# A two-block transformer on one core: in its mixers, a half chunk between the up projections, one gate product ahead of a weight's low part, and the first merged turns ahead of the last branch half

## Chip, cores, metric

One core of a Trainium2 chip runs the whole program. The metric is the device time of one execution in microseconds (us), lower is better.

## What is computed

The input is one sequence of 256 tokens of width 1024 in float32. A first block of two layers is followed by a second block of two layers. The change lies in the token mixer, which each layer of the first block has once:

```
def token_mixer(hn, ...):
    proj = hn @ w_in
    moba_qkv, sb_qkv, c_q, c_kv, k_rope, gates = split(proj)
    y_a = moba_attention(rope(qa), rope(ka), va)
    y_b = stick_breaking_attention(qb, kb, vb)
    qc = rms_norm(c_q, q_norm) @ w_uq
    kv = rms_norm(c_kv, kv_norm) @ w_ukv
    y_c = causal_softmax_attention(qc, [k_nope, rope(k_rope)], vc)
    g = sigmoid(gates + b_gate)
    merged = sum over the 3 branches of (ys @ w_branch) * g
    return merged @ w_out
```

Around it stand, in each layer, two dense feed-forward parts, norms, modulation by a conditioning vector, and gated residuals. The second block has attention and a mixture of 16 experts, and is not touched.

## The kernel before, in words

Every engine has its own instruction stream, written out by hand; semaphores tie them together. The plan is a list of steps (norm, ffn, mixer, backT, out, resid and so on) that each engine walks through in the same order. `b` holds the counts of each semaphore at the start of a step.

Weights arrive as chunks of 128 x 2048 floats (1 MB), by SP's DMA queue, in a ring of six staging buffers. A matmul in full precision is made of three in a reduced one, so each chunk is taken apart first: ACT rounds it to `w_hi` (`hi(n)`, line 699), DVE subtracts that and rounds the rest to `w_lo` (`lo(n)`, line 1363), each for three chunks at a time (PARTS = 3). `chunk_ready` counts the chunks whose low part is done, `pe_used` the chunks PE is through with. Activations are split in the same way (`hT_hi`, `hT_lo`, `yT_hi`, `yT_lo`). `mm3` (lines 2314, 2317, 2318) issues the three matmuls: high by high, high by low weight, low by high weight.

In the mixer chunks 0 to 33 are counted from `b["n"]`. Three places matter here.

**The up projections.** PE multiplies chunks 0 to 3 (latents and the first 512 columns), then `up_q` (chunk 4) for both token tiles, one into two banks of `acc`, one into `gu`, then `up_kv` (chunk 5) into the same banks. Each has to wait until ACT has copied out what `up_q` left there (`pre_out`). Then come chunks 6 and 7, each in two halves, one for each token tile (`half(c, t, ...)`, 12 matmuls into bank `acc[:, 2 + t]`), with turns (transposes) of q and k among them (`m_turns`). ACT's stream has `hi` of chunks 5 and 6, the copies of `up_q` and `up_kv` in PE's order, and behind them `hi` of chunks 7 and 8. DVE's has `lo` of 5 and 6, the rotary products, `lo` of 7, then copies of turned pieces with `lo` of 8 among them. `half_used` counts first halves done, and ACT waits on it before it copies.

**The slots.** 24 slots of attention heads follow. In slot `s_` PE does a head's scores, weights and outputs, and fills in chunk 8 + `s_` by halves (`fill(s_, 0)`, `fill(s_, 1)`). `MIX_FILL` says what a chunk is: "J" a projection, "G" half of a gate's chunk pair, "B" a branch's output. DVE takes each finished sum out of its bank: `take_block(s_, t)` adds the bias for a gate, or, for a branch, multiplies by the gate (line 2063) and adds to the sum over branches (line 2066). PE may write a bank again when `fill_out[t]` has counted that. In slot 19 the block is ("B", 0, 1). There, as in every slot, DVE's `lo(n0 + 8 + s_ + 2)`, here of chunk 29, stands ahead of `take_block(s_, 0)`, and `take_block` is what frees the bank for `fill(20, 0)`. ACT, ahead of chunk 29's high part, does a sigmoid with two loads of its table.

**The end.** After the slots come chunks 32 and 33 (branch 1, two column halves; `MIX_FILL` 24 and 25). `take_block` of them completes `tok`, the merged sum, and counts `mg_ready`, four in all. Step `backT` turns the first half of the columns (rounds 0 and 1, line 2454), which ACT copies out as `hT_hi` (line 777) and DVE as `hT_lo` (line 1396). Step `out` multiplies by w_out: `high_rows` (16 matmuls, line 2431, two banks for each token tile), `low_rows` (8, line 2441), turn rounds 2 and 3, then `rows` of the next chunk. DVE's stream there: `take_block(24, 0)`, `take_block(24, 1)`, `lo` of chunk 34, `take_block(25, 0)`, `take_block(25, 1)`, `lo` of chunk 35, then the low parts of the turns.

Of the kernel before, what the change touches and what calls it, by code (L numbers as in the profile page):

```python
# [16 lines left out]
NT = S // P  # L17
# [279 lines left out]
def build(nc, wstream, ada_stream, c_in, xin, const_in, vec_in, bgate_in, lam_in, rbias_in, t5_in, rel_in, rw_in, out):  # L297
# [14 lines left out]
    with ExitStack() as ctx:  # L312
# [1036 lines left out]
        def _(dve):  # L1349
# [586 lines left out]
            def mixer(b, l):  # L1936
# [144 lines left out]
                for s_ in range(SLOT_HEADS):  # L2081
# [3 lines left out]
                    if s_ == 0:  # L2085
                        divide(0)
                    if s_ < SLOT_HEADS - 1:
                        lo(n0 + MIX_PRE + s_ + 2)
# [4 lines left out]
                    if s_ == SLOT_HEADS - 1:  # L2093
                        argument(s_)
                    if mine:
                        take_block(s_, 0)
# [214 lines left out]
        def _(pe):  # L2311
# [8 lines left out]
            def chunk_wait(n, i=0, rounds=1):  # L2320
                pe.wait_ge(chunk_ready, n + 1 + STAGES * rounds * i)
# [95 lines left out]
            def merged(r):  # L2417

                return [tok[:, t, (2 * r + k) * P:(2 * r + k + 1) * P] for k in range(2) for t in range(NT)]

            def high_rows(n, lhs, turned):

                pe.wait_ge(th_ready, turned)
                chunk_wait(n)
                s = n % PARTS
                for t in range(NT):
                    for k in range(2):
                        for h in range(2):
                            c = slice(k * D + h * 512, k * D + (h + 1) * 512)
                            for w in (w_hi, w_lo):  # L2430
                                pe.matmul(acc[:, 2 * t + h, :], lhs(k, t)[0], w[:, s, c], start=k == 0 and w is w_hi, stop=False,
                                          skip_group_check=True)
# [548 lines left out]
            def mixer(b, l):  # L2981
# [9 lines left out]

                def half(c, t, dst, k0, first, last, src=(hT_hi, hT_lo)):

                    n = n0 + c
                    if t == 0:
                        chunk_wait(n)
                    for k in range(4):
                        cols = slice(k * 512, (k + 1) * 512)
                        ins = mm3(dst, *(v[:, k0 + k, t * P:(t + 1) * P] for v in src), w_hi[:, n % PARTS, cols],
                                  w_lo[:, n % PARTS, cols], first and k == 0, last and k == 3)  # L3000
                    ins.then_inc(pe_used if t else half_used, 1)

# [31 lines left out]
                up_q(1, gu)  # L3034
                chunk_wait(n0 + 5)
                pe.wait_ge(pre_out, b["po"] + 3)
                up_kv(0, acc[:, 0:2, :])
                pe.wait_ge(pre_out, b["po"] + 4)
                up_kv(1, gu)
                half(6, 0, acc[:, 2, :], 0, True, False)  # L3040
                half(6, 1, acc[:, 3, :], 0, True, False)
                pe.wait_ge(rope_ready, 3 * l + 1)
                m_turns(0)
                half(7, 0, acc[:, 2, :], 4, False, True)
                m_turns(2)
# [118 lines left out]
                for s_ in range(SLOT_HEADS, len(MIX_FILL)):  # L3164
                    for t in range(NT):
                        fill(s_, t)

            pe.nop().then_inc(pe_used, PARTS)
            pe.wait_ge(ld, 16 * N_LD)
            for step, b in plan:  # L3170
# [18 lines left out]
                elif kind == "mixer":  # L3189
                    mixer(b, step[1])  # L3190
                elif kind == "backT":
                    pe.wait_ge(mg_ready, b["mg"])
                    for r in range(2):
                        turn(b["u"] + r, merged(r))
                elif kind == "out":
                    def of(c):
                        return lambda k, t: tuple(v[:, 2 * c + k, t * P:(t + 1) * P] for v in (hT_hi, hT_lo))

                    high_rows(b["n"], of(0), b["th"] - 3)
                    pe.wait_ge(tr_free, b["u"] - 1)  # L3200
                    low_rows(b["n"], of(0))
                    for r in range(2, 4):
                        turn(b["u"] - 4 + r, merged(r))
# [222 lines left out]
```

## Time and profile before

| | |
|---|---|
| median of 3 runs | 2117.34 us (2117.26 to 2125.36) |
| the profiled execution | 2117.01 us |
| its span | 2115.2 us |
| mean granted TensorE clock | 0.979 of full speed |
| PE busy (matmuls) | 1975.3 us, 93% |
| DVE busy | 1381.0 us, 65% |
| ACT busy | 848.7 us, 40% |
| chain that ended last | PE 79%, DVE 9%, ACT 5%, DMA 3%, issue 3% |

The span runs from the first to the last instruction; the execution's time has 1.8 us more around it. The share of an engine is its busy time over the span. The first mixer lies between about 240 and 500 us of the span, the second between about 895 and 1160 us.

### The profile page before, as it was taken

To read this page: it belongs to the slowest core of one execution; us is meant where nothing else is said; L and a number is where in the kernel's file an instruction comes from. 1 tells how busy PE (TensorE), PEld (TensorE's weight loads), DVE (VectorE), ACT (ScalarE), POOL (GpSimd) and SP (SyncE) were. 2 spreads that over 40 slices of the span, in tenths; PEclk is the share of its full clock that TensorE was granted. 3 is DMA by queue.
4 is the path that set the end of the run, shared out by engine and by line. 5 is a ranking of instruction groups with operands and counts; after the bars stand their busy time and mean duration, and the time that the engine had idled before them with its cause. 6 is when DMAs were issued, how large, how long until landed. Compare 5 with 4: busy or idle time off the path is not lost.

```text
span 2115.2 us, 25821 instructions
## 1 busy us (share of the span) xinstructions
PE 1975.3 (93%) x9588; PEld 1443.4 (68%) x9588; DVE 1381.0 (65%) x2202; ACT 848.7 (40%) x1127; POOL 63.7 (3%) x95
## 2 busy tenths in 40 slices
PE   3999999998999999999999999998799989889998
PEld 2788777776888788778777788776544447764443
DVE  6899776767888798876776888776511146642112
ACT  3343555655433543464654444564200035421000
POOL 0000000000000000000000000020000001000000
PEclk9999999999999999999999999999899999989999
DMA  9999444435897799754444799762999996359997
GB/s 396 377 372 376 185 174 156 158 125 228 334 372 301 286 365 368 269 189 160 155 145 149 300 368 382 209 225 97 311 422 421 421 350 242 120 217 422 421 421 318
DMA packets 98176, 597.88 MB, mean 283 GB/s; under 512 B 20240, under 2 KB 23696, under 8 KB 27408
## 3 DMA queue, kind: packets, MB, share of 16 engines
q1 hardware_dynamic: 91600, 585.18, 71.2%
q10 hardware_dynamic: 6464, 11.15, 1.6%
q8 instruction: 76, 1.25, 0.2%
q14 instruction: 36, 0.29, 0.0%
HBM read 595.21 MB, written 1.09 MB: 282 GB/s over the span
## 4 chain that ended last, share of the span: by engine, by line
PE 79%; DVE 9%; ACT 5%; DMA 3%; issue 3%; POOL 1%; ACTq 0%; DVEq 0%; POOLq 0%; SPq 0%
PE gu L2704 11%; PE acc L2314 10%; PE acc L2318 10%; PE acc L2317 10%; PE gu L2314 7%; PE tr L2704 7%; PE gu L2318 7%; PE gu L2317 7%; PE tr L2454 3%; PE acc L2704 3%; ACT w_hi L699 2%; DVE w_lo L1363 2%; DMA more_proj<-wstream 1%; DVE tf L2168 1%; DMA lam<-lam_in 1%
## 5 line engine op out<-in xcount | busy, mean ns | idle before, releaser
L1363 DVE TENSOR_TENSOR w_lo<-stage,w_hi 128x2048 fp32r<-128x2048 f32 x232 | 530.4, 2290 | 90.3 <-ACT w_hi L699 89.9
L699 ACT ACTIVATE w_hi<-stage 128x2048 fp32r<-128x2048 f32 x232 | 442.7, 1913 | 210.2 <-PE acc L2318 204.0
L1428 DVE SCALAR_TENSOR_TENSOR proj<-proj,c_row 128x1024 f32<-128x1024 f32 x240 | 292.1, 1221 | 37.3 <-DMA proj<-ada_stream 26.5
L2314 PE MATMUL acc<-w_hi,hT_hi 128*128 128x512 f32 x656 | 270.6, 412 | 5.9 <-DVE z_mix L2063 2.8
L2314 PE MATMUL gu<-w_hi,hT_hi 128*128 128x512 f32 x656 | 261.4, 399 | 13.1 <-DVE pair L1498 10.7
L2318 PE MATMUL acc<-w_hi,hT_lo 128*128 128x512 f32 x656 | 258.1, 393 | 0.0
L2317 PE MATMUL acc<-w_lo,hT_hi 128*128 128x512 f32 x656 | 257.7, 393 | 0.0
L2318 PE MATMUL gu<-w_hi,hT_lo 128*128 128x512 f32 x656 | 257.1, 392 | 0.0
L2317 PE MATMUL gu<-w_lo,hT_hi 128*128 128x512 f32 x656 | 257.0, 392 | 0.0
L2314 PE MATMUL acc<-w_hi,yT_hi 128*128 128x512 f32 (+1 forms) x460 | 180.8, 393 | 2.8 <-ACT proj L1143 2.7
L2318 PE MATMUL acc<-w_hi,yT_lo 128*128 128x512 f32 (+1 forms) x460 | 178.8, 389 | 0.0
L2317 PE MATMUL acc<-w_lo,yT_hi 128*128 128x512 f32 (+1 forms) x460 | 178.6, 388 | 0.0
L2314 PEld LDWEIGHTS gu<-w_hi,hT_hi 128*128 128x128 f32 x656 | 124.0, 189 | 40.5 <-DVE pair L1498 13.2
L2314 PEld LDWEIGHTS acc<-w_hi,hT_hi 128*128 128x128 f32 x656 | 124.4, 190 | 38.9 <-issue 6.6
L2318 PEld LDWEIGHTS acc<-w_hi,hT_lo 128*128 128x128 f32 x656 | 124.3, 189 | 27.7
L2318 PEld LDWEIGHTS gu<-w_hi,hT_lo 128*128 128x128 f32 x656 | 124.0, 189 | 26.7
L2317 PEld LDWEIGHTS gu<-w_lo,hT_hi 128*128 128x128 f32 x656 | 124.1, 189 | 24.6
L2317 PEld LDWEIGHTS acc<-w_lo,hT_hi 128*128 128x128 f32 x656 | 124.7, 190 | 23.0
L1585 DVE TENSOR_TENSOR pair<-pair,gu 128x256 f32<-128x256 f32 x32 | 13.5, 422 | 154.6 <-ACT pair L838 154.6
L2314 PEld LDWEIGHTS acc<-w_hi,yT_hi 128*128 128x128 f32 x460 | 86.4, 188 | 22.5 <-DVE w_lo L1363 3.0
L2318 PEld LDWEIGHTS acc<-w_hi,yT_lo 128*128 128x128 f32 x460 | 86.4, 188 | 18.1
L2317 PEld LDWEIGHTS acc<-w_lo,yT_hi 128*128 128x128 f32 x460 | 86.4, 188 | 17.2
(273 smaller groups left out, 2541.3 us busy)
## 6 DMA issues: line engine op xcount, KB each, us to landing
stage<-wstream SPq DMA_DIRECT2D x312, 1024.0 KB, 5.4
proj<-ada_stream SPq DMA_DIRECT2D x120, 1024.0 KB, 7.5
w_raw<-wstream SPq DMA_DIRECT2D x72, 1024.0 KB, 19.0
z_mix<-wstream SPq DMA_DIRECT2D x12, 1024.0 KB, 16.1
more_yT<-wstream SPq DMA_DIRECT2D x12, 1024.0 KB, 17.4
more_prob<-wstream SPq DMA_DIRECT2D x12, 1024.0 KB, 17.5
more_proj<-wstream SPq DMA_DIRECT2D x12, 1024.0 KB, 19.0
tok<-gate_rows SPq DMA_DIRECT2D x10, 512.0 KB, 4.9
```

The lines of the kernel that those rows point to most:

```text
L699: act.activation(w_hi[:, n % PARTS, :], stage[:, n % STAGES, :], ACT.Copy).then_inc(hi_ready, 1)
L1363: dve.tensor_tensor(w_lo[:, n % PARTS, :], stage[:, n % STAGES, :], w_hi[:, n % PARTS, :].bitcast(F32), ALU.subtract).then_inc(chunk_ready, 1)
L1428: ins = dve.scalar_tensor_tensor(w, w, 1.0, c_row[:], ALU.mult, ALU.mult, accum_out=dst)
L1585: dve.tensor_tensor(both[:, j, BLK:2 * BLK], both[:, j, 0:BLK], gu[:, j, BLK:2 * BLK], ALU.mult).then_inc(both_ready, 1)
L2168: ins = dve.tensor_scalar(tf[:, (b["tf"] + r) % 2, j * P:(j + 1) * P], tr[:, (b["u"] + r) % 2, j * P:(j + 1) * P], mod[:, 3 * k + 1, c:c + ...
L2314: ins = pe.matmul(dst, l_hi, r_hi, start=start, stop=False, skip_group_check=True)
L2317: pe.matmul(dst, l_hi, r_lo, start=False, stop=False, skip_group_check=True)
L2318: return pe.matmul(dst, l_lo, r_hi, start=False, stop=stop, skip_group_check=True)
L2454: ins = pe.transpose(tr[0:rows_, u % 2, j * P:(j + 1) * P], src, ident)
L2704: return pe.matmul(dst, lhs, rhs, start=start, stop=stop, skip_group_check=True)
```

## The change

It has three parts, made in both mixers.

1. PE issues the first half of chunk 6 (`half(6, 0)`) between `up_q` and `up_kv`. It waits for chunk 6 and for the bank that ACT copies out (`pre_out`, count 2). Since half chunks are counted in `half_used`, the half counts nothing there (`done=0`) and that of chunk 7 counts two.
2. DVE does `take_block(19, 0)` ahead of `lo` of chunk 29.
3. PE does turn rounds 0 and 1 of the merged sum ahead of `fill(25, 1)`, the last half. They wait for two of the four counts of `mg_ready` now. `high_rows` waits, ahead of its second token tile, for `fill_out` of both banks, and rounds 2 and 3 wait for all four counts.

```diff
@@ DVE, mixer
+                    early = mine and MIX_FILL[s_] == ("B", 0, 1)
+                    if early:
+                        take_block(s_, 0)
                     if s_ < SLOT_HEADS - 1:
                         lo(n0 + MIX_PRE + s_ + 2)
...
-                    if mine:
+                    if mine and not early:
                         take_block(s_, 0)
@@ PE, high_rows
-            def high_rows(n, lhs, turned):
+            def high_rows(n, lhs, turned, filled):
...
                 for t in range(NT):
+                    if t:
+                        for half in range(2):
+                            pe.wait_ge(fill_out[half], filled)
@@ PE, mixer
-                chunk_wait(n0 + 5)
+                pe.wait_ge(pre_out, b["po"] + 2)
+                half(6, 0, acc[:, 2, :], 0, True, False, done=0)
                 pe.wait_ge(pre_out, b["po"] + 3)
                 up_kv(0, acc[:, 0:2, :])
                 pe.wait_ge(pre_out, b["po"] + 4)
                 up_kv(1, gu)
-                half(6, 0, acc[:, 2, :], 0, True, False)
                 half(6, 1, acc[:, 3, :], 0, True, False)
                 pe.wait_ge(rope_ready, 3 * l + 1)
                 m_turns(0)
-                half(7, 0, acc[:, 2, :], 4, False, True)
+                half(7, 0, acc[:, 2, :], 4, False, True, done=2)
...
-                    for t in range(NT):
+                    for t in range(NT if s_ < len(MIX_FILL) - 1 else 1):
                         fill(s_, t)
+                return lambda: fill(len(MIX_FILL) - 1, 1)
@@ PE, backT and out
-                    pe.wait_ge(mg_ready, b["mg"])
+                    pe.wait_ge(mg_ready, b["mg"] - 2)
                     for r in range(2):
                         turn(b["u"] + r, merged(r))
+                    last_fill()
...
-                    high_rows(b["n"], of(0), b["th"] - 3)
+                    high_rows(b["n"], of(0), b["th"] - 3, b["fo"])
                     pe.wait_ge(tr_free, b["u"] - 1)
                     low_rows(b["n"], of(0))
+                    pe.wait_ge(mg_ready, b["mg"])
                     for r in range(2, 4):
                         turn(b["u"] - 4 + r, merged(r))
```

PE behind the last matmul of `up_q`, before. `yT` is the latents' input (`up_kv`), `hT` that of chunk 6; line numbers of the changed kernel are 3 or 6 higher for the same code.

```order
L2314 MATMUL acc<-w_hi,yT_hi 128x512 [waits pre_out,chunk_ready]
L2317 MATMUL acc<-w_lo,yT_hi 128x512
L2318 MATMUL acc<-w_hi,yT_lo 128x512
...
L2314 MATMUL gu<-w_hi,yT_hi 128x512 [waits pre_out]
...
L2314 MATMUL acc<-w_hi,hT_hi 128x512 [waits chunk_ready]
```

The same place now:

```order
L2317 MATMUL acc<-w_hi,hT_hi 128x512 [waits chunk_ready,pre_out]
L2320 MATMUL acc<-w_lo,hT_hi 128x512
L2321 MATMUL acc<-w_hi,hT_lo 128x512
...
L2317 MATMUL acc<-w_hi,yT_hi 128x512 [waits pre_out]
...
L2317 MATMUL gu<-w_hi,yT_hi 128x512 [waits pre_out]
```

The 12 matmuls of the first half of chunk 6 stand ahead of the 12 of `up_kv`. The wait on `chunk_ready` that stood at `up_kv` was for chunk 5, and is for chunk 6 now. No instruction of ACT moves, and no DMA.

DVE in slot 19, before (line 2004 begins the scores of slot 20, line 2011 the next head's sum):

```order
L2004 SCALAR_TENSOR_TENSOR prob<-gu,const 128x384 [waits p_ready,s_full,dve_up]
L1363 TENSOR_TENSOR w_lo<-stage,w_hi 128x2048 [waits hi_ready]
L2063 TENSOR_TENSOR z_mix<-z_mix,acc 128x512 [waits e_ready,half_used]
L2066 TENSOR_TENSOR tok<-tok,z_mix 128x512 [waits fill_out0]
L2011 SCALAR_TENSOR_TENSOR soft_p<-prob,soft_p 128x384 [waits soft_ready,dve_up]
```

And now:

```order
L2004 SCALAR_TENSOR_TENSOR prob<-gu,const 128x384 [waits p_ready,s_full,dve_up]
L2063 TENSOR_TENSOR z_mix<-z_mix,acc 128x512 [waits e_ready,half_used]
L2066 TENSOR_TENSOR tok<-tok,z_mix 128x512 [waits fill_out0]
L1363 TENSOR_TENSOR w_lo<-stage,w_hi 128x2048 [waits hi_ready,dve_up]
L2011 SCALAR_TENSOR_TENSOR soft_p<-prob,soft_p 128x384 [waits soft_ready]
```

The gate product and its sum stand ahead of the low part of chunk 29.

PE at the end of a mixer, before: the last half (`yT`), the turns (`tok`), `high_rows` (line 2431).

```order
L2314 MATMUL acc<-w_hi,yT_hi 128x512 [waits fill_out1]
...
L2454 MATMUL tr<-const,tok 128x128 [waits tr_free,mg_ready]
L2454 MATMUL tr<-const,tok 128x128 x3
L2454 MATMUL tr<-const,tok 128x128 [waits tr_free]
...
L2431 MATMUL acc<-w_hi,hT_hi 128x512 [waits chunk_ready,th_ready]
```

And now:

```order
L2460 MATMUL tr<-const,tok 128x128 [waits tr_free,mg_ready]
L2460 MATMUL tr<-const,tok 128x128 x3
L2460 MATMUL tr<-const,tok 128x128 [waits tr_free]
...
L2317 MATMUL acc<-w_hi,yT_hi 128x512 [waits fill_out1]
...
L2437 MATMUL acc<-w_hi,hT_hi 128x512 [waits chunk_ready,th_ready]
...
L2437 MATMUL acc<-w_hi,hT_hi 128x512 [waits fill_out1,fill_out0]
```

The eight turns stand ahead of the last half's 12 matmuls, and the second eight matmuls of `high_rows` have waits of their own.

## Rows read from the trace of the kernel before

**Rows 1.** The page: the span, and the costliest line of the mixers' fills (part 5).
```profile
span 2115.2 us, 25821 instructions
...
L2314 PE MATMUL acc<-w_hi,hT_hi 128*128 128x512 f32 x656 | 270.6, 412 | 5.9 <-DVE z_mix L2063 2.8
```

**Rows 2.** Timeline, PE, first mixer's up projections: start, length, engine, line, instruction, [idle before <-releaser].
```profile
269.30 0.28 PE L2318 MATMUL gu<-w_hi,yT_lo 128*128 128x256 f32 x1
...
270.91 0.47 PE L2314 MATMUL acc<-w_hi,yT_hi 128*128 128x512 f32 x1 [1.34 <-ACT proj L1143]
...
273.72 0.39 PE L2314 MATMUL acc<-w_hi,hT_hi 128*128 128x512 f32 x1
...
279.16 1.04 PE L2454 MATMUL tr<-const,proj 128*96 128x128 f32 x8
...
279.95 0.47 PE L2314 MATMUL acc<-w_hi,hT_hi 128*128 128x512 f32 x1
```

**Rows 3.** Timeline, ACT, the same stretch.
```profile
266.36 3.71 ACT L699 ACTIVATE w_hi<-stage 128x2048 fp32r<-128x2048 f32 x2
...
273.92 0.60 ACT L1143 ACTIVATE proj<-gu 128x512 f32<-128x512 f32 x1 [0.27 <-PE gu L2318]
...
274.89 3.73 ACT L699 ACTIVATE w_hi<-stage 128x2048 fp32r<-128x2048 f32 x2
```

**Rows 4.** Timeline, DVE, the same stretch.
```profile
268.31 4.50 DVE L1363 TENSOR_TENSOR w_lo<-stage,w_hi 128x2048 fp32r<-128x2048 f32 x2 [5.01 <-ACT w_hi L699]
...
276.84 2.29 DVE L1363 TENSOR_TENSOR w_lo<-stage,w_hi 128x2048 fp32r<-128x2048 f32 x1 [0.59 <-ACT w_hi L699]
```

**Rows 5.** Timeline, PE, the second mixer's up projections.
```profile
925.94 0.47 PE L2314 MATMUL acc<-w_hi,yT_hi 128*128 128x512 f32 x1 [1.34 <-ACT proj L1143]
```

**Rows 6.** Timeline, PE, DVE and ACT, slot 19 of the first mixer.
```profile
435.47 0.50 PE L2314 MATMUL acc<-w_hi,hT_hi 128*128 128x512 f32 x1 [1.39 <-DVE z_mix L2063]
...
432.52 2.29 DVE L1363 TENSOR_TENSOR w_lo<-stage,w_hi 128x2048 fp32r<-128x2048 f32 x1 [3.85 <-ACT w_hi L699]
...
434.73 0.68 DVE L2063 TENSOR_TENSOR z_mix<-z_mix,acc 128x512 f32<-128x512 f32 x1
...
430.58 1.92 ACT L699 ACTIVATE w_hi<-stage 128x2048 fp32r<-128x2048 f32 x1
```

**Rows 7.** Timeline, PE, slot 19 of the second mixer.
```profile
1090.49 0.50 PE L2314 MATMUL acc<-w_hi,hT_hi 128*128 128x512 f32 x1 [1.39 <-DVE z_mix L2063]
```

**Rows 8.** Timeline, PE, end of the first mixer.
```profile
473.34 0.39 PE L2314 MATMUL acc<-w_hi,yT_hi 128*128 128x512 f32 x1
...
477.73 1.09 PE L2454 MATMUL tr<-const,tok 128*128 128x128 f32 x8 [1.51 <-DVE tok L2066]
...
479.07 0.79 PE L2431 MATMUL acc<-w_hi,hT_hi 128*128 128x512 f32 x1 [0.25 <-ACT hT_hi L777]
...
484.45 1.98 PE L2441 MATMUL acc<-w_hi,hT_lo 128*128 128x512 f32 x8
...
487.07 0.48 PE L2314 MATMUL acc<-w_hi,hT_hi 128*128 128x512 f32 x1
```

**Rows 9.** Timeline, DVE and ACT, end of the first mixer.
```profile
477.60 2.28 DVE L1363 TENSOR_TENSOR w_lo<-stage,w_hi 128x2048 fp32r<-128x2048 f32 x1
...
479.80 1.28 DVE L1396 TENSOR_TENSOR hT_lo<-tr,hT_hi 128x512 fp32r<-128x512 f32 x2
...
478.42 1.09 ACT L777 ACTIVATE hT_hi<-tr 128x512 fp32r<-128x512 f32 x2 [5.62 <-PE tr L2454]
```

**Rows 10.** Timeline, PE, end of the second mixer.
```profile
1132.80 1.09 PE L2454 MATMUL tr<-const,tok 128*128 128x128 f32 x8 [1.50 <-DVE tok L2066]
```

**Rows 11.** Busy time by stretch; the number before the DMA share is the granted clock.
```profile
1445.30:1451.70 6.40, 4.56 (x23) 3.50 (x21) 5.07 (x15) 2.90 (x12) 1.90 (x2) 0.50 0.00 0
...
269.00:273.00 4.00, 2.66 (x14) 2.17 (x14) 4.00 (x4) 2.92 (x4) 0.00 (x0) 1.00 0.27 70
...
479.00:483.00 4.00, 3.93 (x10) 3.19 (x11) 2.08 (x3) 0.51 (x2) 0.00 (x0) 0.57 0.00 0
```

More of the change, by code:

```diff
@@ L2990, in copied, with half @@
                     pe.wait_ge(tr_free, u_of(*what) + 1 + 2)
-                def half(c, t, dst, k0, first, last, src=(hT_hi, hT_lo)):
+                def half(c, t, dst, k0, first, last, src=(hT_hi, hT_lo), done=1):
                     n = n0 + c
@@ L3000, in half @@
                                   w_lo[:, n % PARTS, cols], first and k == 0, last and k == 3)
-                    ins.then_inc(pe_used if t else half_used, 1)
+                    if done:
+                        ins.then_inc(pe_used if t else half_used, done)
                 def up_q(t, pair_):
@@ L3189, in _ @@
                 elif kind == "mixer":
-                    mixer(b, step[1])
+                    last_fill = mixer(b, step[1])
                 elif kind == "backT":
-                    pe.wait_ge(mg_ready, b["mg"])
+                    pe.wait_ge(mg_ready, b["mg"] - 2)
                     for r in range(2):
                         turn(b["u"] + r, merged(r))
+                    last_fill()
                 elif kind == "out":
```

## The prediction

> **What bounds the kernel now.** I read the page first. Its fifth part puts 270.6 us on the first matmuls of the fills into `acc`, and only 5.9 us of idle time before all 656 of them, of which 2.8 us end with DVE's gate product, line 2063 [rows 1]. So TensorE (PE) sets the pace in the mixers, and what a change there can give is the few gaps in its stream. The timeline of one engine at a time shows them, and the releaser in brackets says who ended each. There are three in each mixer, and each part of the change is aimed at one:
>
> - between `up_q` and `up_kv` PE stands for 1.34 us and then waits no longer for ACT's copy [rows 2]; the second mixer has the same 1.34 us [rows 5];
> - in slot 19 it stands for 1.39 us until line 2063 [rows 6], and again 1.39 us in the second mixer [rows 7];
> - at the end it stands for 1.51 us until DVE has the merged sum, does eight turns, and stands again until ACT has copied the first of them [rows 8]; in the second mixer it is 1.50 us [rows 10].
>
> The view of busy time by stretch adds one thing. Over 479 to 483 us the granted clock is 0.57, so nearly all of that stretch ran at the lower level, 1.2 GHz [rows 11]. Ahead of it PE had spent 3.0 us (from 476.06, see below, to 479.07) on nothing but eight turns [rows 8]. Over 269 to 273 us, with the first gap in it, the clock is whole [rows 11].
>
> Two step sizes are used throughout. From 273.72 to 279.16 PE issues 24 matmuls [rows 2], so one takes 0.227 us and a half chunk of 12 takes 2.72 us, or 2.81 us behind a pause, since a first matmul takes longer. The eight turns that begin at 279.16 are over at 279.95 [rows 2], so eight turns are 0.79 us.
>
> **Part 1, the half chunk between the up projections.** It costs no instruction; it moves 12 matmuls ahead of 12. The question is when chunk 6 is ready, because the half waits for that now. ACT's two high parts (chunks 5 and 6) run from 266.36 for 3.71 us [rows 3], and DVE's two low parts from 268.31 for 4.50 us, so chunk 6 is ready at 268.31 + 4.50 = 272.81 [rows 4]. Nothing in front of either moves. The last matmul of `up_q` starts at 269.30 and its 256 columns take half a step, so PE is free at 269.42 and would wait until about 272.90 (PE follows DVE by up to 0.1 us, as 434.73 + 0.68 is followed by 435.47 [rows 6]): 3.5 us in place of 1.5. Before, `up_kv` filled this very time, since chunk 5 is ready 2.2 us earlier. Then:
>
> - the half: 272.90 + 2.81 = 275.71; `up_kv`: + 2.72 = 278.43; `half(6, 1)`: + 2.72 = 281.15, where it was 279.16. The order by itself loses 1.99 us.
> - ACT has its copies of `up_kv` ahead of the high parts of chunks 7 and 8. The copy begins 0.20 us behind PE's last `up_kv` (273.72 to 273.92), the high part at 274.89 [rows 3], the low part at 276.84 and takes 2.29 us [rows 4]. From the end of `up_kv` to chunk 7 for PE that is 1.17 + 1.95 + 2.29 + 0.1 = 5.51 us. Before: 273.72 + 5.51 = 279.23, in time for `half(7, 0)` at 279.95 [rows 2]. Now: 278.43 + 5.51 = 283.94. PE is through with its turns at 281.15 + 0.79 = 281.94 and waits 2.0 us more.
>
> So `half(7, 0)` starts at 283.94, 3.99 us late. What is behind it is chained to it in the same way as before (DVE's low part of chunk 8 waits behind copies of turned pieces), so I let the 3.99 us stand to the end of the mixer. Two mixers: + 7.98 us.
>
> **Part 2, the gate product ahead of the low part.** `fill(19, 0)` is over long before; line 2063 needs only that and the sigmoid, and ACT's next work, the high part of chunk 29, begins at 430.58, behind the sigmoid [rows 6]. That high part holds up the low part, which runs from 432.52; line 2063 stands behind it, at 434.73, and PE starts at 435.47 [rows 6]. Moved ahead, line 2063 and 2066 fit in the time in which DVE waits for the high part (idle 3.85 us; at 0.68 us each the two need 1.4), so the low part loses nothing and PE's 1.39 us go. The next sum's work on DVE moves up by the same 1.4 us, so no new wait stands behind it. Two mixers: - 2.78 us.
>
> **Part 3, turns ahead of the last half.** Before, `fill(25, 1)` starts at 473.34 and is over at 473.34 + 2.72 = 476.06; `rows` of the next chunk starts at 487.07 [rows 8]: 13.73 us. Now, from 473.34: turns 0.79 (their two counts are in, as DVE was through with chunk 32 before), so 474.13; last half 2.81, so 476.94; ACT copies both turns meanwhile, 1.09 us [rows 9]. `high_rows` at full speed: 16 x 0.229 = 3.66 (0.229 is 1.83 us, from 484.45 to eight turns before 487.07, over the 8 matmuls of `low_rows` [rows 8]), so 480.60. `low_rows` needs DVE's first low part of the turns. DVE takes the last block from 477.14 (0.20 us behind PE), 2 x 0.68 us, then chunk 35, which is 2.20 us from 477.60 to 479.80, then 0.68 [rows 9]: ready at 481.48 for PE, a new wait of 0.88 us. Then 1.83 + 0.79 = 484.10. Gain 2.97 us, of which 1.72 are the clock: the 16 matmuls of `high_rows` took 484.45 - 479.07 = 5.38 us [rows 8] against 3.66. Two mixers: - 5.94 us.
>
> **The clock at the new pauses.** These are the unknown. With no fall at all the cost is nothing; with one it is 1.72 us, as just measured. Part 1 leaves two pauses in each mixer: 3.5 us with no instruction at all, longer than the 3.0 us that stood before the low clock at the end; and 2.0 us behind eight turns, 2.8 us in all, just short of it. I take a fall at the first in both mixers and at the second in one of two: 3 x 1.72 = + 5.16 us. The bounds are 0 and 4 x 1.72 = 6.88.
>
> The Trainium skill (TensorE: Matmul & The Clock Gate, "Why this matters for your kernels") advises leaving PE no long idle gap between bursts of matmuls. By its measure the first pause counts and the second does not, two falls, and the sum would be 2119.7. The trace speaks against so mild a reading: the pause at the end that went before a fall had 1.51 us of waiting in one piece and less in the other [rows 8].
>
> **Sum.** + 7.98 - 2.78 - 5.94 + 5.16 = + 4.42 us. The profiled execution took 2117.01 us, 0.33 below the median of the runs, so 2121.4 us: 0.2% more, no change by the 0.5% (10.6 us) that I count as distinguishable.
>
> **Rivals.**
> - *No fall of the clock in part 1* (the first gap, 1.34 us, had none): 2117.01 - 0.74 = 2116.3. Against it speaks the length of the pauses. Chance 0.10.
> - *Only the first pause costs*: chunk 7 isn't late, because something ahead of its high part moves up. Then 2 x 1.99 + 2 x 1.72 - 8.72 = - 1.3, 2115.7. In ACT's order nothing can. Chance 0.08.
> - *The half does fit the gap*, chunk 6 being ready at 269.4. Then `up_kv` ends at 269.42 + 2.81 + 2.72 = 274.95, chunk 7 is ready at 280.46, still 0.5 us late by ACT's order: 2117.01 + 1.0 - 8.72 = 2109.3. Rows 4 speak against it. With a further gain, which I have not found, it would be faster by over 0.5% (under 2106.4). Chance 0.04, of which 0.03 for the latter.
> - *The end gains only its waits*: a fall of the clock comes there too, behind the 0.88 us. 2117.01 + 4.42 + 2 x 1.72 = 2124.9. Chance 0.07.
> - *Slower by over 0.5%*: the clock falls at all four pauses of part 1 and each time stays low twice as long. The trace has one such stretch, 6.4 us at 0.50, with 4.56 us of PE busy in it [rows 11]. Each costs 3.44 in place of 1.72: 7.98 + 13.76 - 2.78 - 5.94 = + 13.0, 2130.0. It decides from 2.9 us for each pause on. Against it: in the mixers PE is busy without a break behind each pause, and at the end the clock was back by 484.45. Chance 0.05.
>
> **How the numbers follow.** The forecast has 0.66; within it all four falls give 2123.2 and two give 2119.7. The range 2115.0 to 2125.0 takes in the first, second and fourth rival and leaves out 0.09. Faster 0.03, same 0.92, slower 0.05: all but the last rival and the far end of the third lie within 0.5%.
>
> **What would show it.** In the profile after: ahead of the half chunk PE idles some 3.3 us, released by line 1363, not by ACT; ahead of `half(7, 0)` a second idle piece of some 2.0 us, again line 1363; line 2063 no longer ends a wait in slot 19; the turns of `tok` have no idle time before them, `high_rows` runs at full clock, and `low_rows` has a wait of 0.8 us for line 1396. A first wait of under 1.5 us would make me wrong on part 1; a low clock behind both pauses of both mixers would put the time at 2123.

## Result and profile after the change

The change takes 2124.26 us in the median of 20 runs (2118.45 to 2127.8), the kernel before 2118.05 us in 20 (2113.34 to 2125.36). The ratio is 1.0025 with a 95% interval of 1.0018 to 1.0032, or + 5.3 us (3.8 to 6.8): no change by the 0.5% bound, though the interval leaves out a difference of nothing, and inside the forecast range. The profiled execution of the change took 2127.80 us, its longest.

The page of the kernel after, parts 1, 4 and 5:

```profile
span 2126.0 us, 25825 instructions
...
PE 1975.1 (93%) x9588; PEld 1442.4 (68%) x9588; DVE 1379.3 (65%) x2202; ACT 847.1 (40%) x1127; POOL 63.5 (3%) x95
...
PE 73%; DVE 12%; DMA 7%; ACT 4%; issue 3%; POOL 1%; SPq 0%; ACTq 0%; DVEq 0%; POOLq 0%
...
L2317 PE MATMUL acc<-w_hi,hT_hi 128*128 128x512 f32 x656 | 271.3, 414 | 12.3 <-DVE w_lo L1363 11.1
```

PE has the same work in the same time. What grew is the idle time ahead of the matmuls of `hT`: 12.3 us in place of 5.9 [rows 1], and 11.1 of them end with line 1363, DVE's low part. In the chain the share of PE fell from 79% to 73%, and that of DVE rose from 9% to 12%; the share of DMA rose as well, from 3% to 7%, but in the mixers the chain passes through no DMA (for the stretch between them see the last point of the section on the prediction).

The timeline of PE after, first mixer's up projections (start, length, engine, line, instruction, [idle before <-releaser]), to be laid beside [rows 2]:

```profile
271.74 0.28 PE L2321 MATMUL gu<-w_hi,yT_lo 128*128 128x256 f32 x1
275.38 0.47 PE L2317 MATMUL acc<-w_hi,hT_hi 128*128 128x512 f32 x1 [3.37 <-DVE w_lo L1363]
...
276.61 0.44 PE L2321 MATMUL acc<-w_hi,hT_lo 128*128 128x512 f32 x1
276.85 0.63 PE L2317 MATMUL acc<-w_hi,hT_hi 128*128 128x512 f32 x1
...
280.25 0.39 PE L2321 MATMUL acc<-w_hi,yT_lo 128*128 128x512 f32 x1
...
285.25 1.03 PE L2460 MATMUL tr<-const,proj 128*96 128x128 f32 x8
287.99 0.50 PE L2317 MATMUL acc<-w_hi,hT_hi 128*128 128x512 f32 x1 [1.71 <-DVE w_lo L1363]
```

Two pauses stand there, 3.37 and 1.71 us, both released by line 1363. Where `up_q` used to be followed by a wait of 1.34 us for ACT, the half chunk waits 3.37 us for chunk 6. The engines that it waits for, after. DVE first:

```profile
270.74 4.49 DVE L1363 TENSOR_TENSOR w_lo<-stage,w_hi 128x2048 fp32r<-128x2048 f32 x2 [5.01 <-ACT w_hi L699]
...
285.64 2.29 DVE L1363 TENSOR_TENSOR w_lo<-stage,w_hi 128x2048 fp32r<-128x2048 f32 x1 [1.30 <-ACT w_hi L699]
```

and ACT:

```profile
282.72 0.60 ACT L1143 ACTIVATE proj<-gu 128x512 f32<-128x512 f32 x1 [0.27 <-PE gu L2321]
...
283.69 3.71 ACT L699 ACTIVATE w_hi<-stage 128x2048 fp32r<-128x2048 f32 x2
```

The two low parts end at 275.23, and PE starts at 275.38. ACT's copies follow `up_kv`, its high part of chunk 7 begins at 283.69, DVE's low part 1.95 us later at 285.64, and PE follows at 287.99: the chain of [rows 3] and [rows 4] step for step, only later.

The windows of the same kernel (length, busy time of PE, PEld, DVE, ACT, POOL with counts, granted clock, DMA share, GB/s) show how the two pauses differ:

```profile
276.80:280.20 3.40, 3.40 (x9) 2.67 (x9) 1.20 (x6) 0.00 (x0) 0.00 (x0) 0.50 0.93 383
...
483.00:487.00 4.00, 4.00 (x19) 3.08 (x17) 3.43 (x3) 0.00 (x0) 0.00 (x0) 1.00 0.00 0
```

Behind the first pause the granted clock is 0.50 for 3.4 us, the lower level, 1.2 GHz; the timeline above has it in the matmuls' lengths, 0.63 us in place of 0.39. Behind the second, from 287.99 on, they stay at 0.39. At the end of the mixer, 483 to 487 us, the clock is whole, where it was 0.57 before [rows 11].

Slot 19 and the end of the mixer, PE after:

```profile
441.98 0.39 PE L2317 MATMUL acc<-w_hi,hT_hi 128*128 128x512 f32 x1
...
483.34 0.39 PE L2437 MATMUL acc<-w_hi,hT_hi 128*128 128x512 f32 x1
...
487.81 2.12 PE L2447 MATMUL acc<-w_hi,hT_lo 128*128 128x512 f32 x8 [0.68 <-DVE hT_lo L1396]
489.76 1.04 PE L2460 MATMUL tr<-const,tok 128*128 128x128 f32 x8
```

In slot 19 the matmul that stood for 1.39 us [rows 6] has no idle time before it. At the end neither the wait for the sum nor that for ACT's copy is left [rows 8]; one of 0.68 us for line 1396 is new.

**How the stretches are measured.** To add this up without the noise of the rest, I cut each mixer into three by PE's own rows: from the first turns (`tr<-const,proj` x6) to the first scores (`gu<-qk`, keys of 96), from there to the start of the last turn of the slots, and from that turn's end to the end of turn rounds 2 and 3. The first in the kernel before:

```profile
259.12 0.82 PE L2454 MATMUL tr<-const,proj 128*128 128x128 f32 x6
...
289.92 1.55 PE L2704 MATMUL gu<-qk 96*128 96x128 f32 x8 [0.87 <-DVE qk L1944]
```

and in the one after:

```profile
261.56 0.81 PE L2460 MATMUL tr<-const,proj 128*128 128x128 f32 x6
...
297.98 1.55 PE L2710 MATMUL gu<-qk 96*128 96x128 f32 x8 [0.87 <-DVE qk L1944]
```

That is 30.80 us before and 36.42 after. All three, for the first mixer (the second agrees within 0.06 us): 30.8, 172.2, 24.9 before; 36.4, 170.5, 22.1 after.

### The profile page after: what moved, and what is told of

It reads as the page before. It is cut to its first block, busy times and chain, and to the rows that moved or that the text cites. A ratio compares the mean times of both kernels' runs of the same rounds, so it can differ in the third digit from the quotient of the medians.

```text
span 2126.0 us, 25825 instructions
## 1 busy us (share of the span) xinstructions
PE 1975.1 (93%) x9588; PEld 1442.4 (68%) x9588; DVE 1379.3 (65%) x2202; ACT 847.1 (40%) x1127; POOL 63.5 (3%) x95
## 4 chain that ended last, share of the span: by engine, by line
PE 73%; DVE 12%; DMA 7%; ACT 4%; issue 3%; POOL 1%; SPq 0%; ACTq 0%; DVEq 0%; POOLq 0%
PE gu L2710 11%; PE acc L2317 10%; PE acc L2321 10%; PE acc L2320 10%; PE tr L2710 7%; PE gu L2317 5%; PE gu L2321 5%; PE gu L2320 5%; DMA proj<-ada_stream 4%; DVE w_lo L1363 4%; PE acc L2710 3%; PE tr L2460 3%; DVE tf L2171 1%; DMA more_proj<-wstream 1%; DVE proj L1428 1%
## 5 line engine op out<-in xcount | busy, mean ns | idle before, releaser
L1428 DVE SCALAR_TENSOR_TENSOR proj<-proj,c_row 128x1024 f32<-128x1024 f32 x240 | 291.7, 1219 | 57.3 <-DMA proj<-ada_stream 47.4
L2317 PE MATMUL acc<-w_hi,hT_hi 128*128 128x512 f32 x656 | 271.3, 414 | 12.3 <-DVE w_lo L1363 11.1
L2317 PE MATMUL gu<-w_hi,hT_hi 128*128 128x512 f32 x656 | 261.4, 399 | 13.2 <-DVE pair L1498 10.8
```

What stands on the lines that cost most here:

```text
L1428: ins = dve.scalar_tensor_tensor(w, w, 1.0, c_row[:], ALU.mult, ALU.mult, accum_out=dst)
L2317: ins = pe.matmul(dst, l_hi, r_hi, start=start, stop=False, skip_group_check=True)
```

## Experiments

"Part 1", "2" and "3" are those of the change. First each part ran alone, and 2 and 3 together. Every ratio is to the kernel before, timed beside the same group of kernels. An interval for the difference in us is that of the ratio, times 2119.

**Part 1 alone.**

```diff
                 up_q(1, gu)
-                chunk_wait(n0 + 5)
+                pe.wait_ge(pre_out, b["po"] + 2)
+                half(6, 0, acc[:, 2, :], 0, True, False, done=0)
                 pe.wait_ge(pre_out, b["po"] + 3)
                 up_kv(0, acc[:, 0:2, :])
                 pe.wait_ge(pre_out, b["po"] + 4)
                 up_kv(1, gu)
-                half(6, 0, acc[:, 2, :], 0, True, False)
...
-                half(7, 0, acc[:, 2, :], 4, False, True)
+                half(7, 0, acc[:, 2, :], 4, False, True, done=2)
```

> Part 1 alone: the kernel before with the half chunk between the up projections. Theory (the half chunk comes before chunk 6 is ready, and ACT's order passes the delay on to chunk 7): 2 x 3.99 us of delay and one fall of the clock per mixer, 2 x 1.7, so 11 us slower than before (9 to 15). In its profile PE stands some 3.4 us in front of the half chunk, released by DVE line 1363, and 1.7 to 2.0 us in front of chunk 7. Rival (the half chunk fills the gap, and what the whole change loses comes from the end of the mixers): 1 to 3 us faster than before.

Measured: 2128.19 us, ratio 1.0047 (1.0033 to 1.0061), + 10.0 us, as the theory had it; the rival, a gain, is refuted. The first stretch is 36.46 us in both mixers, with the fall behind the first pause in both and none behind the second. The end, whose order is that of before, shows a surprise. PE there, in this kernel:

```profile
485.28 1.09 PE L2454 MATMUL tr<-const,tok 128*128 128x128 f32 x8 [1.50 <-DVE tok L2066]
486.62 0.50 PE L2431 MATMUL acc<-w_hi,hT_hi 128*128 128x512 f32 x1 [0.25 <-ACT hT_hi L777]
...
490.38 1.98 PE L2441 MATMUL acc<-w_hi,hT_lo 128*128 128x512 f32 x8
```

The same waits, 1.50 and 0.25 us, and yet the 16 matmuls of `high_rows` take 3.76 us in place of 5.38 [rows 8]: no fall.

**Part 2 alone.**

```diff
+                    early = mine and MIX_FILL[s_] == ("B", 0, 1)
+                    if early:
+                        take_block(s_, 0)
...
-                    if mine:
+                    if mine and not early:
                         take_block(s_, 0)
```

> Part 2 alone: the gate product of slot 19 ahead of the low part of chunk 29. Theory: PE's 1.39 us go in each mixer and nothing takes their place, 2.8 us faster. Rival (the low part or the next head's work becomes late in its place): within 1 us of before, with a new wait of PE in slot 20 or 21.

Measured: 2112.81 us, 0.9968 (0.9955 to 0.9981), - 6.8 us (- 9.5 to - 4.0). The slots take 170.47 us in place of 172.2, and no new wait of PE follows there, so the rival is refuted. But the total gained more than the theory's 2.8 us, and more than the 3.4 us that the slots of two mixers explain. The end has no fall in either mixer, as in part 1 alone, where the profile of before has one in both; two falls less at 1.6 us each would fill the gap. One profile of each kernel can't show that before has them more often, and nothing in part 2 says why it should.

**Part 3 alone** (with the waits in `high_rows` and ahead of turn rounds 2 and 3, as in the diff of the change).

```diff
-                    for t in range(NT):
+                    for t in range(NT if s_ < len(MIX_FILL) - 1 else 1):
                         fill(s_, t)
...
-                    pe.wait_ge(mg_ready, b["mg"])
+                    pe.wait_ge(mg_ready, b["mg"] - 2)
                     for r in range(2):
                         turn(b["u"] + r, merged(r))
+                    last_fill()
```

> Part 3 alone: two rounds of turns ahead of the last half chunk. Theory: 2.97 us less in each mixer, 5.9 us faster, high_rows at full clock, a new wait of 0.7 to 0.9 us for line 1396. Rival (the fall of the clock only moves to the next pause, in the norm behind the mixer): 2.5 us faster, and the profile has a low clock in the norm behind each mixer.

Measured: 2112.10 us, 0.9972 (0.9961 to 0.9983), - 5.9 us (- 8.3 to - 3.6). The end is 22.08 us at full clock, and the profile has no low clock in the norm behind either mixer, which is what the rival needed.

**Parts 2 and 3, without the half chunk** (both diffs above together).

> Parts 2 and 3 without part 1: the half chunk is back behind up_kv. Theory: 8.7 us faster than before, near 2109.5, and so 13 to 15 us faster than the whole change. Rival (the gains don't add up, as the later parts of the program eat them): 4 us faster or less.

Measured: 2110.57 us, 0.9960 (0.9947 to 0.9973), - 8.5 us, as expected; 30.84, 170.45 and 22.08 us. The half chunk is the whole loss: the change without it is faster than before, the change with it slower.

**The change again**, beside two kernels that take one of its pauses away each.

> The whole change, unaltered, beside the three kernels below. The parts by themselves gave + 10.0 (half only) and - 8.5 us (the other two together). If they add up, it is 1 to 3 us slower than before; the first comparison gave + 5.3 (3.8 to 6.8). Theory: some 4.4 us slower, one or two falls of the clock per mixer behind the new pauses; what a single profile shows beyond that is falls of the clock in the norms, which come and go with each execution. Rival (the parts disturb each other): 6 us or more again, at one place that the profile shows.

Measured: 2124.17 us, 1.0026 (1.0013 to 1.0039), + 5.5 us (2.8 to 8.3). The parts by themselves, + 10.0 and - 8.5, add up to + 1.5, and the change came out near + 5.4 twice. Each of these numbers has 1.5 to 3 us of interval to either side, so the difference of 4 us is hardly beyond the noise, and the profile shows no one place for it. Its profile has the fall behind the first pause in one mixer and not in the other, which gives the price of the fall with all else equal. Windows of it, first and second pause of the first mixer, then of the second:

```profile
272.70:276.10 3.40, 3.38 (x15) 2.81 (x16) 2.57 (x12) 0.00 (x0) 0.00 (x0) 1.00 1.00 386
283.70:287.10 3.40, 3.35 (x17) 2.79 (x18) 1.19 (x2) 1.06 (x2) 0.00 (x0) 1.00 0.64 210
928.50:931.90 3.40, 3.37 (x10) 2.70 (x11) 2.58 (x12) 0.00 (x0) 0.00 (x0) 0.68 1.02 424
941.10:945.00 3.90, 3.87 (x21) 3.31 (x22) 1.54 (x3) 1.34 (x2) 0.00 (x0) 1.00 0.65 231
```

The first stretch is 34.84 us without the fall and 36.40 with it: 1.6 us for a fall. The waits are 3.37 and 1.71 us in both.

**First pause filled with work.** 14 matmuls that nobody needs run in the first pause, with chunk 4's weights, into bank `acc[:, 3]`; the second half of chunk 6 overwrites their result.

```diff
                 pe.wait_ge(pre_out, b["po"] + 2)
+                for j in range(14):
+                    pe.matmul(acc[:, 3, :], yT_hi[:, 0, 0:P], w_hi[:, (n0 + 4) % PARTS, 0:512], start=True, stop=True,
+                              skip_group_check=True)
                 half(6, 0, acc[:, 2, :], 0, True, False, done=0)
```

> The change, with 14 more matmuls of 512 columns ahead of the half chunk, into a free bank that the next half overwrites (3.2 us of work in a pause of 3.4). The half chunk starts when it did. Theory: the clock stays whole behind the first pause, and the delay of 3.99 us stays; 3.4 us faster than the whole change. Rival (the low clock costs nothing, since PE waits for chunk 7 afterwards in any case): within 1 us of the whole change, with the second pause longer by what the first saved.

Measured: 2123.44 us, 1.0022 (1.0008 to 1.0036). PE, in this kernel:

```profile
269.58 3.36 PE L3044 MATMUL acc<-w_hi,yT_hi 128*128 128x512 f32 x14
273.02 0.50 PE L2317 MATMUL acc<-w_hi,hT_hi 128*128 128x512 f32 x1
...
275.88 0.39 PE L2317 MATMUL acc<-w_hi,yT_hi 128*128 128x512 f32 x1
...
284.06 0.50 PE L2317 MATMUL acc<-w_hi,hT_hi 128*128 128x512 f32 x1 [1.70 <-DVE w_lo L1363]
```

The fall is gone in both mixers, where the same place had one in 7 of 8 with the pause left empty, and the stretch is 34.76 us. So it is the idle time that brings the fall, and the rest of part 1's cost, 4.0 us, is the later start of the half chunk and of chunk 7. The rival wanted the low clock to cost nothing, as the second pause would grow by what the first saved. It did not grow: 1.70 us here, 1.71 with the fall. The median, though, came only 0.7 us under that of the change again, not 3.4, with intervals that overlap; it lies within the rival's "within 1 us". The total settles nothing, and the stretch decides.

**Chunk 7 ahead of the copies.** ACT rounds chunk 7 before it copies `up_kv` out, and DVE takes its low part ahead of the rotary copies.

```diff
                 up_q(1, gu[:])
+                hi(n0 + 7)
                 half_done_at(5)
                 up_kv(0, acc[:, 0:2, :])
                 used(5)
                 up_kv(1, gu[:])
-                hi(n0 + 7)
...
+                lo(n0 + 7)
                 dve.wait_ge(pre_out, b["po"] + 6)
...
-                lo(n0 + 7)
                 for r in range(4):
```

> The change, with the high part of chunk 7 ahead of ACT's copies of up_kv and its low part ahead of DVE's wait for them. Theory: the wait ahead of half(7, 0) goes, 1.7 to 2.0 us in each mixer, so 3.4 to 4 us faster than the whole change; the first pause of 3.4 us and the fall behind it stay. Rival (something else holds half(7, 0), or the turns that need those copies become late): less than 1 us faster, and a new wait at the turns of k.

Measured: 2117.82 us, 0.9992 (0.9983 to 1.0001). The second pause is gone and the stretch is 34.46 us, 1.97 less, so 3.9 for two mixers as expected, and no new wait stands at the turns of k. The total gained 7 us against the change again. That is more than the stretches explain, but the two intervals, 1.9 and 2.8 us to either side, leave room for 3.9. The first pause keeps its 3.37 us and its fall, in both mixers.

**Chunk 5 into ACT's idle time.** In [rows 3] ACT's high parts begin at 266.36, behind its copy of the first 512 columns. Ahead of that copy ACT stands idle for 2.90 us. So the high part of chunk 5 goes there, ahead of the copy; the kernel has parts 2 and 3, not 1.

```diff
                 take_hi(b, 2, yT_hi, False, (512, 256))
+                hi(n0 + 5)
                 used(3)
                 evac(proj[:, :, 0:512], acc[:, 2:4, :]).then_inc(pre_out, 1)
-                hi(n0 + 5)
                 hi(n0 + 6)
```

> Parts 2 and 3 without part 1, and the high part of chunk 5 moved ahead of ACT's copy of the first 512 columns, into ACT's idle 2.9 us. Theory: the copy of up_q then begins 1.8 us earlier, and PE's 1.34 us between the up projections go without any matmul moved: 3.0 us faster than parts 2 and 3 alone, 11.5 us faster than before (2107). Rival (the wait moves to chunk 6 or to ACT's later copies): as parts 2 and 3 alone, 8.5 us faster than before.

Measured: 2107.89 us, 0.9955 (0.9940 to 0.9969), - 9.5 us: between the theory's 11.5 and the rival's 8.5, and its interval holds both. The rows decide. ACT, in this kernel:

```profile
263.26 1.91 ACT L699 ACTIVATE w_hi<-stage 128x2048 fp32r<-128x2048 f32 x1
266.26 1.03 ACT L1143 ACTIVATE proj<-acc 128x1024 f32<-128x1024 f32 x1 [1.09 <-PE acc L2321]
267.18 1.90 ACT L699 ACTIVATE w_hi<-stage 128x2048 fp32r<-128x2048 f32 x1
268.98 0.80 ACT L1143 ACTIVATE proj<-acc 128x768 f32<-128x768 f32 x1
```

The copy of `up_q`'s first tile begins 2.72 us behind the copy of the first columns, where it was 4.53 us (269.97 against 265.44 before). PE has no idle time left between the up projections, and the stretch is 29.25 us in place of 30.8, so no new wait took the old one's place. This cures the gap that part 1 was aimed at, at its releaser.

**The change with chunk 5 early** (the edit just shown, on the whole change).

> The whole change with the high part of chunk 5 moved ahead of ACT's copy of the first 512 columns, so that chunk 6 is ready 2.2 us earlier. Theory: the half chunk waits 1.1 us in place of 3.4, the clock stays, and chunk 7 is still late by ACT's order: from the first latents' turns to the first scores it takes 32.6 us (before 30.8, the change 34.8 or 36.4, parts 2 and 3 with chunk 5 early 29.2); 3.4 us slower a mixer than without part 1, so some 4.5 us faster than before. Rival (with chunk 6 in time the half chunk is a gain as meant): 29 us or less there, and at least as fast as parts 2 and 3 with chunk 5 early.

Measured: 2116.25 us, 0.9981 (0.9966 to 0.9996), - 4.0 us. PE, in this kernel:

```profile
271.02 0.47 PE L2317 MATMUL acc<-w_hi,hT_hi 128*128 128x512 f32 x1 [1.17 <-DVE w_lo L1363]
...
282.02 0.50 PE L2317 MATMUL acc<-w_hi,hT_hi 128*128 128x512 f32 x1 [1.71 <-DVE w_lo L1363]
```

The first pause is down to 1.17 us, with no fall behind it, and the stretch is 32.61 us, as the theory had it.

**And chunk 7 first too** (the edits for chunks 5 and 7 on the whole change).

> The one before, and the high and low parts of chunk 7 ahead of the copies of up_kv as well: both waits that part 1 made are shortened. Theory: 30.6 us in the stretch of the up projections, 1.1 us of it the wait for chunk 6; 8.5 us faster than before, and still 2.5 us slower than e11's kernel without its last edit. Rival (a third wait appears at the turns of k, as the copies of up_kv are late): above 31.5 us.

Measured: 2111.20 us, 0.9958 (0.9942 to 0.9973), - 8.9 us; the stretch is 30.64 us. With the second pause gone and the first cut to 1.17 us, part 1 still loses 1.4 us in each mixer against the kernel with chunk 5 early and no half chunk (29.25). There is no gap left for the half chunk to fill.

**The low part of chunk 35 between the turns' low parts**, against the 0.68 us at the end, on parts 2 and 3 with chunk 5 early.

```diff
                 for r in range(rounds):
+                    if between is not None and r == 2:
+                        lo(between)
...
-                    lo(n0 + MIX_CHUNKS + s_ - SLOT_HEADS)
+                    if s_ == SLOT_HEADS:
+                        lo(n0 + MIX_CHUNKS)
...
-                    take_lo(b, 4, hT_hi, hT_lo)
+                    take_lo(b, 4, hT_hi, hT_lo, between=b["n"] + 1)
```

> Parts 2 and 3, chunk 5 early, and DVE's low part of chunk 35 behind the low parts of turn rounds 0 and 1. Theory: the wait of 0.68 us ahead of low_rows goes in each mixer, the end takes 21.4 us in place of 22.06, and it is 1.4 us faster than the kernel below. Rival (chunk 35 becomes late for rows in its place): the end takes 22 us or more, with a wait for line 1363.

Measured: 2110.67 us, 0.9953 (0.9934 to 0.9971), - 10.0 us. The wait is gone and the end is 21.08 us, 0.98 less, but the total shows nothing of it beside the kernel below, whose interval holds it. It is too small for this many runs.

**Parts 2 and 3 with chunk 5 early, again**, timed beside the last three.

> Parts 2 and 3 with chunk 5 early, again, beside the three others. Theory: 10 us faster than before (local sum: 2 x 1.55 + 2 x 1.7 + 2 x 1.27 = 9.0, and 1.6 for each fall of the clock at the end of a mixer that before has and this has not). Rival (the first run was a lucky one): 7 us or less.

Measured: 2109.52 us, 0.9941 (0.9922 to 0.9960), - 12.5 us; the rival, 7 us or less, is outside. Together with its first run (0.9955) it is the kernel to keep: faster than the one before by 0.4 to 0.6%, and faster than the change.

All runs in one table. "By the stretches" is the sum over both mixers of the three stretches of its own profile against those of before; its two ends take before's end as 24.9 us (with a fall, as in before's profile) and as 23.3 (without, as with parts 1 and 2 alone, which keep before's end). "Measured" is (ratio - 1) x 2119.

| kernel | first stretch, us | slots | end | by the stretches | measured |
|---|---|---|---|---|---|
| before | 30.8 | 172.2 | 24.9 | | |
| change | 36.4 | 170.5 | 22.1 | + 2.1 to + 5.3 | + 5.3 |
| part 1 | 36.5 | 172.2 | 23.3 | + 8.1 to + 11.3 | + 10.0 |
| part 2 | 30.8 | 170.5 | 23.3 | - 6.6 to - 3.4 | - 6.8 |
| part 3 | 30.8 | 172.2 | 22.1 | - 5.7 to - 2.4 | - 5.9 |
| parts 2, 3 | 30.8 | 170.5 | 22.1 | - 9.1 to - 5.8 | - 8.5 |
| change again | 34.8 and 36.4 | 170.5 | 22.1 | + 0.4 to + 3.7 | + 5.5 |
| pause filled | 34.8 | 170.5 | 22.1 | - 1.2 to + 2.0 | + 4.7 |
| chunk 7 first | 34.5 | 170.5 | 22.1 | - 1.9 to + 1.3 | - 1.7 |
| 2, 3, chunk 5 early | 29.2 | 170.5 | 22.1 | - 12.3 to - 9.0 | - 9.5, again - 12.5 |
| change, chunk 5 early | 32.6 | 170.5 | 22.1 | - 5.6 to - 2.3 | - 4.0 |
| and chunk 7 first | 30.6 | 170.5 | 22.1 | - 9.6 to - 6.3 | - 8.9 |
| low part later | 29.2 | 170.5 | 21.1 | - 14.2 to - 11.0 | - 10.0 |

Half an interval is 1.5 to 4 us in each line. Eleven of the thirteen timed medians lie inside their bounds or within 1 us of them. The other two are above them: the change again by 1.8 us and the filled pause by 2.7. So the three stretches account for the totals as well as these can be measured. Whether part 1 costs something outside them, up to 3 us by those two, stays open. On average over the thirteen the measured value stands 2.0 us above its lower bound and 1.3 below its upper, which would fit ends that fall in before in some four cases of ten.

**Falls in the norm behind a mixer.** The table leaves these out, and they are an open end. In the 28 mixers profiled, 13 have a low clock in the norm that follows. 6 of them cost 1.6 us, and 7 cost nothing. The kernel before has one of the second kind, behind its second mixer. Its two norms, the first without a fall and the second with one:

```profile
506.93 0.47 PE L2353 MATMUL gu<-w_hi,hT_hi 128*128 128x512 f32 x1 [1.60 <-ACT hT_hi L1286]
...
511.85 0.66 PE L2330 MATMUL tr<-const,tok 128*128 128x128 f32 x4 [1.34 <-ACT tok L1269]
...
1161.99 0.76 PE L2353 MATMUL gu<-w_hi,hT_hi 128*128 128x512 f32 x1 [1.60 <-ACT hT_hi L1286]
...
1166.92 0.66 PE L2330 MATMUL tr<-const,tok 128*128 128x128 f32 x4 [0.44 <-ACT tok L1269]
```

From the first matmul to the turns it is 4.92 us without the fall and 4.93 with it: the wait of 1.34 us shrank to 0.44 and, with a shorter one before it, took up what the slow matmuls lost. In the change's norms the fall comes later, where no wait follows, and costs its 1.6 us in both. The three kernels without part 3 have 1 of the 13 in 6 mixers, those with it 12 in 22. That is too few to say whether part 3, which takes PE's idle time at the end away, brings them on; if it does, the 6 that cost something make 0.9 us for two mixers.

## Why the prediction held, step by step

- *Part 1's order and waits, + 3.99 us for each mixer*: right, 34.84 - 30.80 = 4.04 us where no fall adds to it. The waits came as 3.37 us (forecast 3.5) and 1.71 us (forecast 2.0), the chain by ACT and DVE as worked out. The kernel with chunk 7 first isolates the second: 1.97 us.
- *Part 2, - 1.39 us for each*: the wait went, and the slots gave 1.7. The 0.3 beyond the idle time lies in how a gap is counted. The rows of slot 19 in the kernel before have the matmul ahead of the gap at 433.69, lasting 0.39 us, and the one behind it at 435.47, which is 1.78 us between two starts. Without a gap two starts are 0.227 apart, so the gap costs 1.55, not the 1.39 that the row calls idle. The first matmul behind it is followed after 0.34 us, 0.11 more than a step. Together 1.66; the forecast left both out. The gap of 1.34 us between the up projections gave 1.55 for the same reason when it was cured.
- *Part 3, - 2.97 us for each, 1.72 of them clock*: the mechanism held, and the new wait was 0.68 us (forecast 0.88). Against an end with a fall the gain is 24.95 - 22.06 = 2.89 us. But I took the fall as always there, because the one profile of before has it in both mixers. Four more ends of the same order, in parts 1 and 2 alone, have none: 2 of 6 in all. Without a fall part 3 gives 23.33 - 22.06 = 1.27. With 1.6 us for a fall and 2 in 6, it is 1.8 on average, and my term of - 5.94 would be - 3.6. This correction isn't sure. The 2 of 6 stand in one execution of three, and part 3 alone measured - 5.9 us (- 8.3 to - 3.6), my own term to the tenth, with - 3.6 at the edge. How often before falls there can only be counted in more profiles of before.
- *Clock at the new pauses, 3 falls at 1.72 us*: one fall too many. Behind the first pause it came in 7 of 8 mixers (the change, part 1 alone, the change again, chunk 7 first), behind the second in none of 10 (the first three, the filled pause, the change with chunk 5 early), and its price was 1.6 us (the forecast's 1.72 held 0.1 for the slower first matmul behind a wait: with no fall the 16 matmuls took 3.76 us, not 3.66). So + 5.16 should have been 2 x 7/8 x 1.6 = + 2.8. I had argued against the rule of the Trainium skill (TensorE: Matmul & The Clock Gate, "Why this matters for your kernels"), by which the first pause counts and the second does not. The runs side with the page, and my counter-evidence, the fall behind 1.51 us of waiting and eight turns, is the same one that came in only 2 of 6. These two, and those in the norms behind 1.60 us of waiting, are falls that its measure does not foresee.
- *The sum*: with the measured terms 2 x 4.04 - 2 x 1.7 - 3.6 + 2.8 = + 3.9 us, and measured were + 5.3 (3.8 to 6.8). The forecast of + 4.42 agrees, partly by luck, because two errors cancelled: the end gave 2.3 less than forecast, the clock took 2.4 less. If the end gave its full 5.8, the sum is + 1.7, and 3.6 us of the measured loss have no place in the stretches. Then only something outside the terms made up for the clock's 2.4. I also added the 4.42 to the profiled execution, 2117.01; added to the median of before, 2117.34, it is 2121.8.
- *Rivals*: that the half fits the gap is refuted by its wait of 3.37 us; that no fall comes, that the end gains only its waits by a new fall, and that all four pauses fall for longer, are each refuted by the profile of the change, whose two mixers have one fall each, behind the first pause. That only the first pause costs is half right, for the clock; chunk 7 was late all the same.
- The profiled executions differ by 10.8 us, twice the 5.3 of the ratio. The mixers hold 2 x (5.6 - 1.7 - 2.9) = 2.0 of that. The change's profile is 2.4 us late before its first mixer (261.56 against 259.12). From the end of the first mixer to the first turns of the second it takes 6.5 us more; 1.6 of them are the fall in the norm, and the second norm has another 1.6. Over the other twelve profiles that piece is 0.1 us shorter to 4.8 us longer than in before, 1.3 in the change again and 3.9 in part 2 alone, so most of the 6.5 belongs to the execution. In the change's profile the chain that ended last passes through DMA for 15.6% of that piece (`proj<-ada_stream`, which DVE's line 1428 waits for), in before's not at all, and in the change again not either. DVE's waits for it over the whole program are 47.4 us against 26.5. Part 1 alone has 26.5 again, so they are not part 1's. But the change again has 46.4, and of the eleven profiles with part 3 nine have 37.8 to 48.4, where the three without it have 26.5 to 29.5. Whether part 3 lengthens them isn't shown.

## What to carry to other kernels

Before work is moved into an engine's gap, look up when the moved work's own inputs are ready, and what stands in order behind the displaced work on the other engines: here the gap was 1.3 us, the moved half chunk was ready 2 us after it, and the displaced `up_kv` held back a copy, a high part and a low part that the next chunk needed. A gap is better cured at its releaser; one line moved into ACT's idle time took it away and gave 1.6 us for each mixer (30.84 to 29.25). A gap costs more than its idle time, here 1.55 to 1.66 us for one of 1.34 or 1.39. And a fall of the clock in one profile is one draw: count it over several before it enters a sum as certain.

## What the runs showed of the hardware that I had not expected

- The same idle pattern, 1.50 us of waiting, eight turns, 0.25 us of waiting, is followed by a lower clock in 2 ends of 6, both in one execution. A pause of 3.37 us is followed by one in 7 of 8 mixers. So whether a fall comes is not settled by the pause's length alone; what else decides was not tried.
- 1.71 us of idle time behind eight turns had no fall in any of 10 mixers, although with the turns before it the time without full-size matmuls, 2.7 us, is nearly that of the end's pattern (3.0 us). In 5 of the 10 another fall had come some 11 us earlier, so these are not ten free draws.
- Each fall in the mixers lasts 3.4 us at the lower level. In the stretches of the up projections and of the end it costs 1.6 us; in the norm behind the second mixer of before it costs 0.01 us, since a wait for ACT follows that takes it up.
